# Token tables of the looped expert tiles read once and shifted, and expert weight loads held until the first gather has landed

## The reference, cut to what matters

```python
for layer in range(DEPTH):                      # DEPTH = 2
    ...                                         # attention of the layer, x = x + gate * out
    h = modulate(rmsnorm(x, norm_ffn[layer]), shift, scale)
    x = x + gate_f * grouped_moe(h, w_router, router_bias, w_gate[layer], w_up[layer], w_down[layer])

def grouped_moe(h, ...):
    scores = sigmoid(h @ w_router)              # (T, 16)
    ...                                         # best group of 4, best 2 experts in it
    gates = one_hot(top_e) * w_sel              # two gates per token, normalised
    act = silu(h @ w_gate[e]) * (h @ w_up[e]) * gates
    return act @ w_down                         # summed over the token's experts
y = rmsnorm(x, norm_final)
```

## Time and profile before

| | |
|---|---|
| profiled execution | 1454.78 us |
| span in the trace, first to last instruction | 1453.0 us |
| median of three runs | 1450.78 us (1449.85 to 1451.74) |
| PE busy | 1280.0 us, 88% |
| DVE / ACT / POOL busy | 554.7 / 341.1 / 270.3 us |
| DMA | 268.98 MB, 185 GB/s over the span |
| tiles of layer 0 / layer 1 | about 519 to 751 us / 1210 to 1436 us |

### The profile page before, as it was taken

One profiled execution on the slowest core, in us unless ns is written; L12 is line 12 of the kernel. 1 busy time (PEld: TensorE's weight loads), 2 busy tenths in 40 slices (PEclk: granted clock), 3 DMA queues, 4 the chain that ended last, 5 costly groups with the idle time before them and its releaser, 6 DMA issues.

```text
span 1453.0 us, 18959 instructions
## 1 busy us (share of the span) xinstructions
PE 1280.0 (88%) x7270; PEld 737.5 (51%) x7270; DVE 554.7 (38%) x1435; ACT 341.1 (23%) x823; POOL 270.3 (19%) x360
## 2 busy tenths in 40 slices
PE   2799899999999859999929999999998985999991
PEld 2565466666655434444414455556775444444440
DVE  2221244444535554444411000003663564444443
ACT  3121244434412200010123000003663320000111
POOL 6110500010010043222220100014121003422221
PEclk9999999999999869999969999999999996999996
DMA  7612211122464568999670372144223536899955
GB/s 277 241 70 90 110 59 59 59 69 108 165 248 173 191 259 304 382 369 312 177 222 28 129 263 117 59 165 162 60 53 105 235 127 250 307 381 373 317 139 189
DMA packets 47701, 268.98 MB, mean 185 GB/s; under 512 B 9036, under 2 KB 15596, under 8 KB 33900
## 3 DMA queue, kind: packets, MB, share of 16 engines
q1 hardware_dynamic: 22588, 192.87, 34.4%
q0 software_dynamic: 19264, 53.93, 13.6%
q10 hardware_dynamic: 5760, 20.97, 3.7%
HBM read 231.28 MB, written 34.88 MB: 183 GB/s over the span
## 4 chain that ended last, share of the span: by engine, by line
PE 79%; DMA 6%; DVE 5%; issue 4%; ACT 4%; ACTq 0%; POOL 0%; POOLq 0%; DVEq 0%; PEldq 0%
PE PS L1073 16%; PE PS L819 12%; PE PS L1160 10%; PE PS L1032 10%; PE PS L724 9%; PE PS L1090 7%; PE PS L938 4%; PE PS L736 3%; PE PS L969 2%; DMA resid<-in_x 2%; DMA info<-slots 2%; PE PS L897 2%; PE PS L979 1%; ACT weights L1421 1%; PE PS L939 1%
## 5 line engine op out<-in xcount | busy, mean ns | idle before, releaser
L724 PE MATMUL PS<-const,big 128*128 128x128 f32 (+2 forms) x643 | 98.2, 293 | 67.2 <-ACT big L1262 28.2
L1032 PE MATMUL PS<-weights,ht 128*128 128x512 f32 x320 | 140.8, 594 | 2.3 <-DVE ht L1556 1.6
L1160 PE MATMUL PS<-ht,weights 128*128 128x128 f32 (+1 forms) x512 | 140.2, 434 | 1.5 <-PE PS L736 0.9
L724 PEld LDWEIGHTS PS<-const,big 128*128 128x128 f32 (+2 forms) x643 | 81.4, 149 | 114.5 <-issue 75.6
L819 PE MATMUL PS<-weights,ht 128*128 128x336 f32 (+1 forms) x320 | 121.6, 539 | 5.9 <-DVE ht L1646 2.4
L1073 PE MATMUL PS<-big 128*128 128x512 f32 x256 | 116.6, 609 | 3.2 <-DVE big L1952 2.3
L1160 PEld LDWEIGHTS PS<-ht,weights 128*128 128x128 f32 x512 | 77.8, 191 | 64.1 <-issue 64.1
L1032 PEld LDWEIGHTS PS<-weights,ht 128*128 128x128 f32 x320 | 59.5, 190 | 72.2 <-issue 72.2
L521 POOL DMA_DIRECT2D modrows<-modrow x32 | 18.3, 574 | 400.1 <-DVE modrow L1556 282.5
L819 PEld LDWEIGHTS PS<-weights,ht 128*128 128x128 f32 x320 | 62.2, 198 | 59.4 <-issue 43.4
L1470 ACT ACTIVATE big<-PS 128x256 f32<-128x256 f32 x34 | 13.1, 385 | 331.5 <-PE PS L1073 331.5
(11 more groups left out here) (219 smaller groups left out, 1826.0 us busy)
## 6 DMA issues: line engine op xcount, KB each, us to landing
weights<-in_ada SPq DMA_DIRECT2D x24, 2048.0 KB, 8.3
big<-in_gu SPq DMA_DIRECT2D x16, 2048.0 KB, 12.9
weights<-in_gu SPq DMA_DIRECT2D x12, 2048.0 KB, 13.6
rows<-in_down SPq DMA_DIRECT2D x18, 1024.0 KB, 7.2
weights<-in_down SPq DMA_DIRECT2D x16, 1024.0 KB, 7.3
ht<-in_gu SPq DMA_DIRECT2D x6, 2048.0 KB
weights<-in_qkv SPq DMA_DIRECT2D x6, 2048.0 KB, 11.7
weights<-in_wo SPq DMA_DIRECT2D x4, 2048.0 KB, 8.7
```

The source lines that it names most:

```text
L724: return pe.transpose(dst, src, const[0:n, C_ID:C_ID + n])
L1032: ins = pe.matmul(bank(4 + j), OT[:, k, t * P:(t + 1) * P], w[j][:, k, :], start=(k == 0), stop=(k == KD - 1))
L1160: ins = pe.matmul(bank(bb, n1 - n0), w[:, k, m * P:(m + 1) * P], hT[:, k, n0:n1], start=(k == 0), stop=(k == KD - 1))
```

## The change

Four things, all in both layers:

1. The 13 tiles of the table from tile 14 on are read by two DMAs on ACT's queue, once, during tile 6, into `last[0]` (used by POOL) and `last[1]` (used by DVE), each 128 x 13 x 2 words. The loop on POOL and on DVE takes its columns from there; at the end of a pass each engine moves its own copy by two tiles (two copies of 22 words per row). POOL's `tokens_in` in the loop and behind it are gone, and of the 16 reads ahead of tile 3 twelve are left.
2. SP waits for the landing of the layer's first gather (`e_gi[l][0]` at 16) before the weight loads that stood around it; in layer 0 that is ahead of `load_gu(2)`, in layer 1 ahead of `load_dn(1)`.
3. In layer 0 `load_dn(2)` stands ahead of `load_gu(3)`.
4. In DVE's loop the copy of the transposed activation (`acts_T`) stands ahead of `y_out`.

```diff
                 load_dn(0)
-                load_dn(1)
+                if l == 0:
+                    load_dn(1)
+                sp.wait_ge(e_gi[l][0], 16)
+                if l == 1:
+                    load_dn(1)
                 sp.wait_ge(w_used[0], static_done(0))
                 load_gu(2)
+                sp.wait_ge(n_hd, 2 * hrow(f"f{l}", NT))
+                load_dn(2)
                 if l == 0:
                     sp.wait_ge(w_used[1], static_done(1))
                     load_gu(3)
-                sp.wait_ge(n_hd, 2 * hrow(f"f{l}", NT))
-                load_dn(2)
                 load_dn(3)
...
-                for n in range(4, STAT + 2):
+                for n in range(4, STAT):
                     tokens_in(slice(n * P, (n + 1) * P), 2 * n, e_inf[l][1])
-                for j in range(2):
-                    n = STAT + j
-                    tokens_in(slice(n * P, (n + 1) * P), 34 + 2 * j, e_gt[l][j])
...
                 with pool.Fori(0, trips) as i:
                     for j in range(2):
...
                         pool.wait_ge(e_tr[l], i * 2 + (STAT + 1 + j))
                         pool.nop().then_inc(e_gate, 1)
-                        rows_of(STAT + j, 1 - j)
-                        pool.wait_ge(e_ac[l], i * 2 + (STAT + 1 + j))
-                        pool.wait_ge(e_gr[l], i * 6 + 3 * (STAT + 1 + j))
-                        pool.nop().then_inc(e_gate, 1)
-                        tokens_in(rows, 34 + 2 * j, e_gt[l][j])
+                        rows_of(last_token(3 + j), 1 - j)
                         pool.wait_ge(e_yd[l], i * 2 + (STAT + j))
                         pool.wait_ge(e_ys[l][1 - j], i * 16 + (112, 128)[j])
                         pool.nop().then_inc(e_gate, 1)
-                        add_rows(38 + 2 * j, j)
+                        add_rows(last_token(j), j)
+                    pool.wait_ge(e_ys[l][1], i * 16 + 16 * 8)
+                    pool.wait_ge(e_gi[l][0], i * 16 + 16 * 10)
+                    pool.nop().then_inc(e_gate, 1)
+                    pool.tensor_copy(moved[0], last[0][:, 4:26]).then_inc(e_next[l], 1)
...
+                    pool.tensor_copy(last[0][:, 0:22], moved[0]).then_inc(e_next[l], 1)
...
+                    if n == 6:
+                        act.wait_ge(rr_sc, 160 * (l + 1))
+                        for v in last:
+                            act.dma_start(v.rearrange("p (n c) -> p n c", c=2),
+                                          slotD[l][(STAT - 1) * P:(STAT + 12) * P, :].rearrange("(n p) c -> p n c", p=P)).then_inc(e_tab[l], 16)
...
                         rows_T(i * 2 + (STAT + 2 + j))
-                        y_out(i * 2 + (STAT + j), i * 6 + 3 * (STAT + j), j, i * 16 + 16 * 7)
                         acts_T(i * 2 + (STAT + 1 + j))
+                        y_out(i * 2 + (STAT + j), i * 8 + 3 * (STAT + j), j, i * 16 + 16 * 7)
```

More of the change, by code:

```diff
@@ L208, in build @@
         grow = big(512, D)
+        last = [big(1536 + i * 32, 26) for i in range(2)]
+        moved = [big(1600 + i * 32, 22) for i in range(2)]
         vecs = big(7000, P)
@@ L300, in build @@
         DNS = (4, 4, 3, 3)
-        e_gw, e_dw, e_inf, e_gt, e_gi, e_ys = ([[sem(f"moe{l}_{n}{i}") for i in range(2)] for l in range(DEPTH)] for n in (
-            "gateup_in", "down_in", "tokens_in", "gates_in", "rows_in", "y_stored"))
+        e_gw, e_dw, e_inf, e_gi, e_ys = ([[sem(f"moe{l}_{n}{i}") for i in range(2)] for l in range(DEPTH)] for n in (
+            "gateup_in", "down_in", "tokens_in", "rows_in", "y_stored"))
+        e_tab, e_next = ([sem(f"moe{l}_{n}") for l in range(DEPTH)] for n in ("last_tiles_in", "last_tiles_moved"))
         c_in = [sem(f"x_back{t}") for t in range(NT)]
@@ L652, in _, with add_rows, last_token @@
                 tokens_in(slice(3 * P, 4 * P), 6, e_inf[l][0])
-                for n in range(4, STAT + 2):
+                for n in range(4, STAT):
                     tokens_in(slice(n * P, (n + 1) * P), 2 * n, e_inf[l][1])
-                for j in range(2):
-                    n = STAT + j
-                    tokens_in(slice(n * P, (n + 1) * P), 34 + 2 * j, e_gt[l][j])
-                def add_rows(at, par):
-                    pool.indirect_dma_start(xD[l], bass.IndirectOffsetOnAxis(ap=info[:, at:at + 1].bitcast(U32), axis=0),
+                def add_rows(token, par):
+                    pool.indirect_dma_start(xD[l], bass.IndirectOffsetOnAxis(ap=token.bitcast(U32), axis=0),
                                             yb[par], None, compute_op=ALU.add).then_inc(e_ys[l][par], 16)
+                def last_token(n):
+                    return last[0][:, 2 * n:2 * n + 1]
                 def add_static(n):
@@ L1952, in rows_T, with acts @@
                     dve.tensor_copy(gatT[:, 4:8, :], bank(4).rearrange("p (c n) -> p c n", c=4)).then_inc(e_td[l], 1)
-                def acts(at, ready, free):
+                def acts(gate, ready, free):
                     dve.wait_ge(e_sg[l], ready)
@@ L1960, in acts @@
                         dve.wait_ge(e_at[l], free)
-                    dve.scalar_tensor_tensor(out=actv, in0=sig, scalar=info[:, at:at + 1], in1=bank(0, DE, DE),
+                    dve.scalar_tensor_tensor(out=actv, in0=sig, scalar=gate, in1=bank(0, DE, DE),
                                              op0=ALU.mult, op1=ALU.mult).then_inc(e_ac[l], 1)
@@ L1966, in acts_T, with gate_rows @@
                     dve.tensor_copy(actT, bank(5, DE).rearrange("p (c n) -> p c n", c=2)).then_inc(e_ae[l], 1)
-                def gate_rows(at, first, second):
-                    tok = info[:, at:at + 1].bitcast(U32)
+                def gate_rows(token, first, second):
+                    tok = token.bitcast(U32)
                     dve.tensor_scalar(rs_[:, 120:121], tok, float(CTX * P), None, ALU.is_lt)
@@ L1991, in moe @@
                     if n == 4:
-                        dve.wait_ge(e_inf[l][1], 16 * 13)
-                    acts(2 * n + 1, n + 1, n or None)
+                        dve.wait_ge(e_inf[l][1], 16 * 11)
+                    acts(info[:, 2 * n + 1:2 * n + 2], n + 1, n or None)
                     if n == 0:
```

52 lines of the change are left out of this document (26 added, 26 removed).

## The result

The changed kernel took 1466.70 us (median of 4 runs, 1464.02 to 1468.59) where the kernel before took 1451.13 beside it (4 runs). The ratio is 1.0107, with a 95% interval of 1.0088 to 1.0126. I had forecast 1438.7 us, and a range that ended at 1446.0.

A forecast was written before the change was run, and what follows sets the result against it. PE was busy 1280.0 of 1453.0 us, so only its waits at tile starts and ends could move. 1.5 + 3.4 + 4.6 + 2.6 = 12.1 us won gave a median of 1438.7 us, range 1432.5 to 1446.

The forecast's parts named there:

- What bounds the kernel: Whole kernel: PE busy 1280.0 of 1453.0 us; the change can move only its 173 us of waiting, at tile starts and ends.
- The first gather in 3.9 us, DVE's copy behind its table: Expert tile starts: gather lands in 3.9 us, DVE's table then comes last; 3.6 us won in layer 0, 3.97 in layer 1.
- What the held loads then collide with: Behind the first gather: scatters cost nothing, third gather 0.6 us per layer, fourth 1.5 in layer 0, 0 in layer 1.
- the two starts: Start of the expert tiles in each layer: 1.5 us won in layer 0, 3.4 us in layer 1.
- Rival 1: Tile starts: contention only moves, loads crowd POOL's queue; starts -1.5 and 0.4 us, 6.1 us won in all, 1444.7 us; chance 0.18.
- Rival 3: Tiles: ACT's 8-byte table pieces each take a turn with loads, gather 15 waits; about 13 us lost per layer, 1464.7 us; chance 0.07.
- ACT's table DMAs at nothing: Tile 6, both layers: issuing the two table DMAs costs nothing, at most 8.6 us, covered by ACT's idle 9.93 us.
- End of layer 0, 4.6 us: Last adds of layer 0 without table reads between: last add issued at 740.4 instead of 745.05, 4.6 us won, between -0.8 and 7.
- End of layer 1, 2.6 us: Last adds of layer 1, no attention loads: last add at 1427.3 instead of 1429.93, 2.6 us won, 2 to 3.
- The reordered copies, `load_dn(2)`: DVE's loop and layer 0's load order: both at nothing; PE's wait has the same sum, and both loads have over 20 us.

The follow-up runs named there:

- e2: Kernel before the change with only the hold and its order of loads, 16 table reads as before: 1468.5 us, ratio 1.0116.
- e11: Changed kernel with its hold, but one table DMA per layer instead of two, DVE copying its columns on chip: 1461.9 us, ratio 1.0079.
- e4: Changed kernel with a staged hold: only tile 2's load (layer 1 also `load_dn(1)`) behind the first gather, others after the table reads ahead of tile 4: 1466.1 us.
- e10: Kernel e7 with the next block's attention loads waiting until the last add of layer 0 has landed: 1450.4 us, ratio 0.9985.
- e14: Changed kernel with only half the columns of each held expert block loaded, for times alone: 1465.1 us, ratio 1.0078.
- e9: Kernel e7 with the staged hold of e4: 1448.1 us, ratio 0.9969.
- e7: Changed kernel without hold, old load order, one table DMA per layer on ACT, DVE copying its columns on chip: 1447.0 us, ratio 0.9960.
- e1: Changed kernel with the old order of weight loads and no hold, keeping the two table DMAs on ACT: 1452.2 us, ratio 1.0000.

## Why the prediction was wrong, step by step

- **What bounds the kernel**: right. PE's busy time changed by 2.0 us of 1280.0, and both starts and ends moved.
- **The first gather in 3.9 us, DVE's copy behind its table**: right. It took 4.4 us (issued 515.38, SP released at 519.8), and the copy moved by 3.8 against the gather's issue, forecast 3.6.
- **What the held loads then collide with** (the term of the two starts): this step failed. I took the scatters at nothing, the third gather at 0 to 0.6 us and the fourth at 0 to 4.5. Measured: scatters 10.77 us to land behind the last issue, the third gather 14.0 us in flight where I took 8.69 as the crowded bound, PE waiting 2.29 and 8.10 us for these two gathers in layer 0, the table reads ahead of the fourth begun only at 542.85, the start at +12.1 where the term said -1.5, and in layer 1 +4.3 for -3.4. e2 and e11 pin it on the hold. I had weighed the gather's own stretch, which was full, and not the 12 us behind it, which were empty and in which the scatters ran. And I had no term for PE's clock, which fell behind two of the waits and made 3.3 us of layer 0's loss. And the 416 GB/s by which I made the loads last 20.2 us is a rate of loads alone: with scatters in flight they ran at 195 to 316.
- **Rival 1** had this mechanism and priced it 6.0 us above the forecast. The starts came out 21.3 us above the forecast (+16.4 for -4.9).
- **Rival 3**: that each piece of 8 bytes is its own packet is right (queue 10's count), and in e4 gather 15 waited as described. In the kernel after the table landed in time. That rival 3's total, 1464.7 us, lies within 2.0 us of the measured 1466.7 is luck: the loss was at the starts.
- **ACT's table DMAs at nothing**: wrong, by another way than those I bounded. I bounded 0 to 8.6 us of issue, under a cover of 9.93. It was 2.10 us in layer 0 and 15.46 in layer 1: 2.9 us lost, 7.2 without the hold.
- **End of layer 0, 4.6 us**: 1.1, with add 15 at 12.1 us in flight, near the crowded end that I had and did not take. e10 shows the cause. The bound of 14.0 from the kernel before gives -0.8, nearer to 1.1 than 4.6 is.
- **End of layer 1, 2.6 us**: 1.9. The mechanism was right, and `y_out` with its copy was 0.7 longer.
- **The reordered copies, `load_dn(2)`**: no wait of PE was put down to either. I did not try them apart.

The Trainium skill (DMA: Bandwidth & Descriptors, Queues, rings and completion order) has the engines take turns between queues by whole packets. The counts agree in the kernel after, 188 of the loads against 160 of POOL from 531 to 539, and less well in e14, 307 against 180. It doesn't say that the loads' own bytes per us fall, as 195 GB/s at a share of 0.95 shows, and I have no run for why.

## What to carry to other kernels

Before loads are held back to free a transfer, look at the DMA share of the 20 us behind it: the held bytes take the room of whatever runs there, and a chain of small dependent DMAs paid 6 to 14 us for each link here. If the stage behind has a DMA share of 1, the delay can come back there: e9 won 8.8 us at the starts and lost 11.2 in the tiles. The full hold cost 15 us; with one table DMA, the staged hold and that of one load neither gained nor lost clearly (1448.1 and 1442.7 against 1447.0). And where two engines need the same table in 8-byte pieces, one DMA and a copy on chip was 5 us faster than two DMAs (e7 and e1).

## What the hardware showed that I had not expected

- A queue instruction on ACT can take 15 to 26 us: two DMAs of 1664 pieces took 1.1 to 2.3 us in layer 0 and 15.46, 18.13, 21.60, 22.72, 23.86 and 25.64 in layer 1 of six kernels; one of them took 0.38 in both.
- Weight loads slow down beside 8-byte scatters: 195 to 316 GB/s at a share of 0.82 to 1.18, with scatters that hold the engines for 1.5% of the time, and 390 to 433 once the scatters have landed.
- A wait of PE can cost more than its length. In the kernel after its granted clock was 1.00 (2.4 GHz) until 536.5 us and 0.50 (1.2 GHz) from there to about 540, behind an idle time of 2.70 us (0.69 is the mean of 535 to 539), and gate/up of tile 1 took 8.72 us in place of 7.11. It was 0.50 from 564 to 570.7 too, in and behind the wait of 8.10 us. In and behind the wait of 2.29 us ahead of 547.72 it stayed at 1.00.
